# Expert gate rows and closing-norm vectors: spread over partitions by TensorE products in place of broadcasting DMAs

## What is computed

```python
def _post_norm(x, out, gain, bias):
    return _layernorm(DEEPNORM_ALPHA * x + out) * gain + bias

for i in range(DEPTH):
    sh_a, sc_a, g_a, sh_f, sc_f, g_f = _ada(c, w_ada[i], b_ada[i])   # c_ctx for the context tokens
    h = _modulate(x, sh_a, sc_a)
    ...                                                              # out: attention or Fourier mixing
    x = _post_norm(x, g_a * out, ln_gain[i, 0], ln_bias[i, 0])
    h = _modulate(x, sh_f, sc_f)
    moe = _hier_moe(h, w_router_group[i], w_router_expert[i], w_expert_gate[i], w_expert_up[i], w_expert_down[i])
    x = _post_norm(x, g_f * moe, ln_gain[i, 1], ln_bias[i, 1])
```

## Time and profile before

| | |
|---|---|
| median of 3 runs | 975.96 us (973.7 to 977.57) |
| profiled execution, span from first to last instruction | 968.9 us |
| PE, DVE, ACT, POOL busy | 821.1, 339.3, 147.5, 176.8 us |
| DMA | 321.39 MB, mean 332 GB/s |
| layer 0's pairs | from 320 us |
| layer 1's pairs | from 702 to 928 us |

### The profile page before, as it was taken

One profiled execution on the slowest core, in us unless ns is written; L12 is line 12 of the kernel. 1 busy time (PEld: TensorE's weight loads), 2 busy tenths in 40 slices (PEclk: granted clock), 3 DMA queues, 4 the chain that ended last, 5 costly groups with the idle time before them and its releaser, 6 DMA issues. The chain is left out here.

```text
span 968.9 us, 12777 instructions
## 1 busy us (share of the span) xinstructions
PE 821.1 (85%) x4895; PEld 419.4 (43%) x4895; DVE 339.3 (35%) x818; ACT 147.5 (15%) x339; POOL 176.8 (18%) x250
## 2 busy tenths in 40 slices
PE   3899999998898897998869788999599987777783
PEld 2555666665457433333323234546433333333331
DVE  3113554556587211111111137848611111101036
ACT  1122222223200111111101012001111110101013
POOL 2041212123122211122111100223212211111100
PEclk9999999999997999999999999999699999999998
DMA  9998493439339897999999979976899999999971
GB/s 333 365 371 305 140 386 112 167 135 342 145 105 387 353 412 290 420 420 418 419 418 419 418 304 356 381 264 230 353 387 418 417 419 418 419 419 420 419 297 65
DMA packets 91020, 321.39 MB, mean 332 GB/s; under 512 B 12686, under 2 KB 25710, under 8 KB 66872
## 3 DMA queue, kind: packets, MB, share of 16 engines
q1 hardware_dynamic: 74400, 289.41, 75.7%
q0 software_dynamic: 12704, 21.86, 6.3%
q10 hardware_dynamic: 3832, 8.99, 2.5%
HBM read 313.62 MB, written 28.90 MB: 354 GB/s over the span
## 5 line engine op out<-in xcount | busy, mean ns | idle before, releaser
L1067 PE MATMUL psum<-ring,arena 128*64 128x512 f32 x880 | 255.2, 629 | 39.1 <-DMA ring<-in_w_expert_up 28.4
L1067 PEld LDWEIGHTS psum<-ring,arena 128*64 128x64 f32 x880 | 84.8, 145 | 169.4 <-issue 166.0
L1089 PE MATMUL psum<-ring,arena 128*64 128x512 f32 x440 | 124.1, 598 | 20.2 <-DVE arena L1883 19.6
L1879 DVE TENSOR_TENSOR arena<-arena,psum 128x256 f32<-128x256 f32 x34 | 14.3, 421 | 283.6 <-ACT arena L1408 277.0
L1067 PE MATMUL psum<-h_hT,arena 128*64 128x512 f32 x208 | 93.1, 601 | 6.0 <-DMA ring<-in_w_expert_up 5.1
L937 PE MATMUL psum<-ring,h_hT 128*128 128x384 f32 x288 | 96.5, 488 | 0.0
L883 PE MATMUL psum<-ring,h_hT 128*128 128x512 f32 x160 | 69.3, 593 | 1.8 <-ACT h_hT L1489 1.5
L684 POOL DMA_INDIRECT y_scratch<-arena,sidx x32 | 33.6, 1048 | 203.9 <-DVE arena L1889 203.9
L937 PEld LDWEIGHTS psum<-ring,h_hT 128*128 128x128 f32 x288 | 53.6, 191 | 34.1
L1089 PEld LDWEIGHTS psum<-ring,arena 128*64 128x64 f32 x440 | 35.6, 136 | 71.2 <-issue 46.8
L1889 DVE COPY arena<-psum 128x512 f32<-128x512 f32 x32 | 22.1, 692 | 120.6 <-PE psum L1089 120.6
(11 more groups left out here) (230 smaller groups left out, 890.0 us busy)
## 6 DMA issues: line engine op xcount, KB each, us to landing
ring<-in_w_expert_down SPq DMA_DIRECT2D x52, 1024.0 KB, 20.6
ring<-in_w_expert_gate SPq DMA_DIRECT2D x50, 1024.0 KB, 19.0
ring<-in_w_expert_up SPq DMA_DIRECT2D x50, 1024.0 KB, 22.2
ring<-in_w_ada SPq DMA_DIRECT2D x24, 2048.0 KB, 15.0
h_hT<-in_w_expert_gate SPq DMA_DIRECT2D x12, 1024.0 KB, 20.4
h_hT<-in_w_expert_up SPq DMA_DIRECT2D x12, 1024.0 KB, 24.0
h_hT<-in_w_expert_down SPq DMA_DIRECT2D x12, 1024.0 KB, 26.5
ring<-in_w_qkv SPq DMA_DIRECT2D x9, 1024.0 KB, 12.5
```

Of the source, the lines that this page charges most:

```text
L1067: last = pe.matmul(bank[b][64 * e:64 * e + 64, :].rearrange("p (g n) -> p g n", g=2), mem.GT[b][:, c, 64 * e:64 * e + 64], w, start=(c == ...
L1089: last = pe.matmul(bank[5 + half][64 * e:64 * e + 64, :], mem.actT[b][:, f, 64 * e:64 * e + 64], w[:, f, 512 * half:512 * half + 512], sta ...
L1879: V.tensor_tensor(mem.act[b], mem.sil[b], bank[b][:, FE:2 * FE], ALU.mult).then_inc(S["act"], 1)
```

## The change

Per layer, the four 512 KB broadcasts go. POOL fetches the two gate rows (`fetch_gates`) and ScalarE the gain and bias as eight rows of 512 numbers into eight partitions of memory that is free by then (`mem.vectors`); both wait for the layer's last normalised rows (`norm_ready`). In pairs 4 to 11 TensorE runs one more product, with row r of an 8 by 8 identity, repeated 128 times, as the stationary side: it puts row r of the eight on all 128 partitions of bank 7. ScalarE copies bank 7 to its place in `gates` or `gb`. Also, gathers and scatters of the regular passes take their row numbers straight from the tables, without copy and wait; those of the extra passes keep both.

```diff
+        self.vectors = self.lnscale[0:8, TOK:TOK + 512]
...
             def gather(S, l, col, n, b):
-                pool.tensor_copy(mem.gidx[:, b:b + 1], mem.tokens[:, bass.ds(col, 1)]).then_inc(S["gidx"], 1)
-                n1 = value(n + 1)
-                pool.wait_ge(S["gidx"], n1)
+                if b == 2:
+                    pool.tensor_copy(mem.gidx[:, b:b + 1], mem.tokens[:, bass.ds(col, 1)]).then_inc(S["gidx"], 1)
+                    n1 = value(n + 1)
+                    pool.wait_ge(S["gidx"], n1)
+                    rows = mem.gidx[:, b:b + 1]
+                else:
+                    rows = mem.tokens[:, col:col + 1]
...
+            def fetch_gates(l):
+
+                pool.wait_ge(norm_ready, 6 * l + 6)
+                for i in range(2):
+                    pool.dma_start(mem.vectors[2 * i:2 * i + 2, :], m_dram[l, i, 5 * D:6 * D].rearrange("(h n) -> h n", h=2)
+                                   ).then_inc(gate_rows_in, 16)
...
                 if l == 0:
-                    pool.wait_ge(proj_used, 6)
-                    for i in range(2):
-                        spread(mem.gates[:, i, :], 0, 5, i, gates_in[i])
+                    fetch_gates(0)
...
                     if n < LAST:
                         gt(S, n + 1, 16 * ((n + 1) // 2 + 1), 1 - b)
+                    if 0 <= n - FIRST_SPREAD < VECTORS:
+                        spread_vector(VECTORS * l + n - FIRST_SPREAD)
                     act_transposes(S, n, b)
...
+                def spread_vector(v):
+
+                    pe.wait_ge(gate_rows_in, 32 * (l + 1))
+                    pe.wait_ge(norm_vectors_in, 32 * (l + 1))
+                    if v >= 1:
+                        pe.wait_ge(spread_sb, v)
+                    r = v % VECTORS
+                    pe.matmul(bank[7], bc(ident[0:VECTORS, r:r + 1], [VECTORS, P]), mem.vectors, start=True, stop=True
+                              ).then_inc(spread_ps, 1)
...
-                load_norm(2 * l + 1)
+                act.wait_ge(norm_ready, 6 * l + 6)
+                for i, name in enumerate(("ln_gain", "ln_bias")):
+                    act.dma_start(mem.vectors[4 + 2 * i:6 + 2 * i, :], A[name][l, 1].rearrange("(h n) -> h n", h=2)
+                                  ).then_inc(norm_vectors_in, 16)
...
                         gt_evict(S, n + 1, 1 - b)
+                        if 0 <= n - FIRST_SPREAD < VECTORS:
+                            vector_evict(n - FIRST_SPREAD)
                         o_evict(S, n, b)
...
             def gates_of_slots(l):
-                for i in range(2):
-                    dve.wait_ge(gates_in[i], 16 * (2 * l + 2))
+                dve.wait_ge(spread_sb, VECTORS * (l + 1))
```

More of the change, by code:

```diff
@@ L345, in build @@
         gate_up_through, down_through = sem("gate_up_through"), sem("down_through")
+        gate_rows_in, norm_vectors_in, spread_ps, spread_sb = (
+            sem(n) for n in ("gate_rows_in", "norm_vectors_in", "spread_ps", "spread_sb"))
         dve_chain, pool_chain = sem("dve_chain"), sem("pool_chain")
         def moe_sems(tag, fetches):
-            names = ("sidx", "gidx", *fetches, "gt_ps", "gt_act", "gt_dve", "u_ps", "sil", "act", "at_ps", "at_sb", "d_ps",
+            names = (*(("sidx", "gidx") if tag == "extra" else ()), *fetches, "gt_ps", "gt_act", "gt_dve", "u_ps", "sil", "act", "at_ps", "at_sb", "d_ps",
                      "o_act", "o_dve", "scattered", "o_free")
@@ L389, in build @@
         OFFSET_BANKS = (4, 0)
+        FIRST_SPREAD, VECTORS = 4, 8
         SUM_BANKS = (((2, 3), (4, 7), (0, 1)), ((2, 3), (0, 1), (6, 7)))
@@ L665, in gather @@
             def gather(S, l, col, n, b):
-                pool.tensor_copy(mem.gidx[:, b:b + 1], mem.tokens[:, bass.ds(col, 1)]).then_inc(S["gidx"], 1)
-                n1 = value(n + 1)
-                pool.wait_ge(S["gidx"], n1)
+                if b == 2:
[5 more added lines that the diff above has]
+                    rows = mem.tokens[:, col:col + 1]
                 pool.sem_inc(turns, 1)
                 pool.indirect_dma_start(mem.G[b], None, h_dram[l],
-                                        bass.IndirectOffsetOnAxis(ap=mem.gidx[:, b:b + 1].bitcast(U32), axis=0),
+                                        bass.IndirectOffsetOnAxis(ap=rows.bitcast(U32), axis=0),
                                         bounds_check=in_bound, oob_is_err=False
@@ L676, in scatter @@
             def scatter(S, l, col, n, b):
-                pool.tensor_copy(mem.sidx[:, b:b + 1], mem.table[:, bass.ds(col, 1)]).then_inc(S["sidx"], 1)
-                n1, n2 = value(n + 1), value(n + 2)
-                pool.wait_ge(S["sidx"], n1)
+                n2 = value(n + 2)
+                if S is extra:
+                    pool.tensor_copy(mem.sidx[:, b:b + 1], mem.table[:, bass.ds(col, 1)]).then_inc(S["sidx"], 1)
+                    n1 = value(n + 1)
+                    pool.wait_ge(S["sidx"], n1)
+                    rows = mem.sidx[:, b:b + 1]
+                else:
+                    rows = mem.table[:, col:col + 1]
                 pool.wait_ge(S["o_act"], n2)
@@ L684, in scatter @@
                 pool.indirect_dma_start(y_dram[l],
-                                        bass.IndirectOffsetOnAxis(ap=mem.sidx[:, b:b + 1].bitcast(U32), axis=0),
+                                        bass.IndirectOffsetOnAxis(ap=rows.bitcast(U32), axis=0),
                                         mem.O[b], None, bounds_check=out_bound, oob_is_err=False
@@ L1304, in head_evict, with load_norm @@
                 nc.scalar.copy(mem.hT[:, k, :], bank[3][:, 0:TOK]).then_inc(head_sb, 1)
[L1306 to L1309 removed]
+            def load_norm(l):
+                if l == 1:
+                    act.wait_ge(gb_used, 2)
                 for i, name in enumerate(("ln_gain", "ln_bias")):
[L1311 removed]
+                    act.dma_start(mem.gb[:, i, :], A[name][l, 0].partition_broadcast(P)).then_inc(gb_in, 16)
             for i, src in enumerate((A["c_ctx"].rearrange("(k p) -> k p", p=P),
@@ L1456, in first, with vector_evict @@
                         scale_rows()
+                def vector_evict(r):
+                    if r == 0:
+                        act.wait_ge(proj_used, 6 * l + 6)
+                        act.wait_ge(gb_used, 2 * l + 1)
+                    act.wait_ge(spread_ps, VECTORS * l + r + 1)
+                    dst, half = (mem.gates, mem.gb)[r // 4][:, r // 2 % 2, :], r % 2
+                    nc.scalar.copy(dst[:, 512 * half:512 * half + 512], bank[7]).then_inc(spread_sb, 1)
                 def body(n, b, r, k):
```

13 lines of the change are left out of this document (6 added, 7 removed).

## The result

| | before | after |
|---|---|---|
| median | 976.21 us (6 runs, 972.96 to 977.88) | 968.85 us (6 runs, 967.10 to 971.08) |
| ratio, 95% interval | | 0.9942 [0.9926, 0.9958] |
| profiled execution: span | 968.9 us | 968.7 us (its own time 970.48) |
| PE, DVE, ACT, POOL busy | 821.1, 339.3, 147.5, 176.8 us | 843.2, 341.3, 156.5, 162.3 us |
| DMA | 321.39 MB, mean 332 GB/s | 317.24 MB, mean 327 GB/s |

By the ratio the changed kernel gains 5.7 us (4.1 to 7.2); the two medians alone differ by 7.4. Forecast were 3.0 us, 973.0, in a range from 969.0 to 977.0. In a second comparison on another chip the ratio was 0.9947 [0.9928, 0.9965], 5.2 us (3.4 to 7.0), before 974.26 (22 runs), after 969.65 (6 runs). So the sign and the order were right.

What follows compares the result with a forecast made beforehand. Bound taken: a handshake of weight loads and TensorE, with DMA full inside the pairs but with holes elsewhere. Sum 1.08 + 1.92 + 0 + 0 = 3.0 us, 975.96 to 973.0, range 969.0 to 977.0.

Steps and rivals of the forecast that it cites:

- Holes, not bytes: Removed broadcasts, 4.19 MB, travel ahead of stretches where DMA runs low: directly they give nothing, only an earlier first gather.
- the microsecond that was named as the test: Prediction is wrong if the pair stages, from first full stretch to their end, change length by more than a microsecond.
- Bytes count: Rival, 6%: all 4.19 MB save time at 418 GB/s, 10.0 us, giving 966.0.
- Layer 1's start: TensorE's 1.92 us idle for layer 1's first gather goes whole; 1.26 kept as the lower end.
- lower bound of 1.26: Layer 1's first gather, issued at the copy's start with its old latency, lands 1.26 us earlier.
- Landing does not move: Rival, 14%: other weights fill the freed time and the gather lands as late as now; 0 to 1 us, about 975.5.
- Layer 0's start: TensorE's 1.08 us idle for layer 0's first gather goes whole, the gather being issued 1.26 us earlier.
- Overflow passes: Layer 0's pairs 0 to 2: first gather's saving is taken back by the second; 0 taken, bounds 0 to 1.0 us more.
- Products: Sixteen products in pairs 4 to 11 delay down products 0.43 to 0.6 us each, covered: 0 taken, 9.6 us uncovered.
- Moves with the work: Rise to full clock in layer 1's first gate_up shifts with the work, so the 1.92 us gain stays whole.
- Early clock: Rival, 16%: layer 1's first gate_up at full clock almost from its start, overflow keeps some saving; up to 6.8 us, 969.2.
- 7.1 us lie around the span: Base of the sum: median 975.96 against profiled span 968.9 us, the difference taken as unchanged.

Runs made afterwards that it cites:

- late_broadcasts: Kernel before without the regular index copies, each layer's four broadcasts asked for in pair 4 instead of at the layer's start; 979.72 us, ratio 1.0050 to before.
- norm_later: Kernel before with layer 1's gain and bias broadcasts asked for behind both first gathers, all bytes and copies kept; 974.40 us, ratio 0.9982.
- copies_only: Kernel before with the index copies of the regular passes removed, broadcasts kept; 973.32 us, ratio 0.9993 to before.
- spread_only: Changed kernel with the index copies and their waits put back, spread products kept; 970.86 us, ratio 0.9974 to before.

## Why the prediction was right, and where it was not

**Holes, not bytes.** Right. The pair stages kept their length within the microsecond that was named as the test: 0.5 us shorter in layer 0, 0.7 longer in layer 1's pairs 1 to 14 (198.4 against 197.6 and 197.8). 10.0 us of transfer left, 5 to 6 of time came, and late_broadcasts shows both prices of the same bytes. "Bytes count" is out.

**Layer 1's start.** Right in kind, 1.92 forecast, 2.4 measured: the rows came from an execution with a short wait (2.82 for the stage against 3.73 in the second profile). The floor behind it, TensorE's own chain through VectorE, was named and is what ends last now. The lower bound of 1.26 "from the new issue" was wrong twice: the request moves by 0.53 us, not 1.21 (the second gather's by 1.1 to 1.2, not 2), and moving it does not move the landing. "Landing does not move" is out, but for the copies alone it is what happens.

**Layer 0's start.** 1.08 forecast, 1.0 in the means, with a scatter as large: norm_later, whose layer 0 is that of before, shows 0.98 without any change. The prediction credited the copies; copies_only has 1.63 and spread_only 0.98, but beside norm_later's 0.98 a single profile of each does not settle which half it is, or whether it is the change at all.

**Overflow passes.** Here a term failed: "I take 0, since the later wait is the one that ends last". The first gather's wait did fall, and the second's did not rise to take it back:

```profile
378.34 1.16 PE L1067 MATMUL psum<-k_rows_sb,arena 128*128 128x128 f32 x8 [0.19 <-DMA arena<-h_scratch,gidx]
```

0.19 after, 0.21 before. The gather of the extra pass keeps its copy, but one of a scatter ahead of it on POOL's queue is gone: it is asked for 3.70 us after the gate and up products ahead of that wait begin, and 4.18 before. About 0.4 us, up to the 1.0 of the bound.

**Products.** Right that they are covered; the price of one was too low (0.88, not 0.43 to 0.6), which cost nothing.

**Clock.** "Moves with the work" holds at layer 1's start: 9.59, 9.87 and 8.94 us for the first gate_up in the three profiles after, 9.83 and 8.98 before. "Early clock" is out.

**End of layer 0.** This had no term and is the largest miss. From pair 14 to the Fourier products six profiles with one or two spread products in layer 0 take 39.36 to 41.01 us, mean 39.9; seven without take 40.50 to 43.03, mean 41.5. The kernel without products moves the same bytes as the changed one and is among the seven, which speaks for the products and against the bytes, by one profile. The difference lies behind SyncE's request for the experts' sums: up to it both groups take 18.8 to 19.3 us (norm_later 20.57), and from it to the Fourier products 20.5 to 20.6 with products (21.75 in the changed kernel's second profile) against 21.2 to 22.8 without. In that second part six of the seven profiles without have a while at half speed, and none of the six with them. First the kernel with four copies and the one without products,

```profile
585.53 3.55 PE L1147 MATMUL psum<-x,k_rows_sb 128*128 128x512 f32 x4 [3.08 <-DVE x L1946]
```

```profile
595.95 3.39 PE L848 MATMUL psum<-ring,silu 128*32 128x128 f32 x64 [2.46 <-DMA ring<-in_w_ada]
```

then the same products in the third profile of the changed kernel:

```profile
587.26 1.98 PE L1169 MATMUL psum<-x,k_rows_sb 128*128 128x512 f32 x4 [0.38 <-DVE x L1982]
...
595.31 1.95 PE L848 MATMUL psum<-ring,silu 128*32 128x128 f32 x64 [0.92 <-DMA ring<-in_w_ada]
```

The granted clock over the first two is 0.54 and 0.56, over the others 1.00; in the six it lengthens the products in this place by 1.4 to 1.8 us, as much as the two means differ. The seventh, the second profile of before, has none and takes 21.2; there, as in three more without products, the last of the sums lands 11.0 to 11.2 us after the first request and not 9.9 to 10.4. So the step that is missing is the clock, which the prediction followed at layer 1's start alone. Why the half speed falls into this place in one group and only ahead of it in the other, and whether the products or chance put it there, was not settled.

**Layer 1 behind its start** gave back about 0.9 us; with profiles of before 0.8 apart there, that stays open. Adding 0.5 for layer 1's start, 0.4 to 1.0 for the overflow passes and 0.8 to 1.6 for the end of layer 0 to the forecast 3.0, and taking off that 0.9, gives 3.8 to 5.2, from just under the first measured interval (4.1 to 7.2) to the lower half of it, and inside the second (3.4 to 7.0).

**Base.** "7.1 us lie around the span" was wrong: 1.8 us do. The rest was the luck of the profiled execution ahead of the experts. The difference did not use it, but the waits of that execution stood for typical ones.

## What to carry to other kernels

Before counting a saved transfer, look for the next stretch in which the DMA engines run dry: bytes ahead of it buy only what an event behind them (here a gather) gains, and the same bytes inside a full stretch buy their whole time. A small indirect transfer behind a loaded queue lands when the load has drained; asked for 0.5 us earlier or 0.7 later, it came at the same moment here, so take away what stands ahead of it. Moving it behind won the start as well, but in the total that did not show (norm_later). Where weights bound a stage, TensorE work put into it is free up to the wait that it replaces, and that limit is found by running it two and four times. And where a sum of waits leaves a microsecond or two over, compare the granted clock of the same products in both kernels.

## What the hardware showed that was not expected

**The clock falls behind products of eight rows, with TensorE busy.** With four products in a pair the granted clock goes to half (1.2 of 2.4 GHz) behind them in each of layer 0's pairs 4 to 11, and with two in pairs 4, 5, 8 and 10, although TensorE has no idle around them beyond waits of half a microsecond. With one it stays at 1.00 through pair 4 in two profiles of the changed kernel and falls in the third (below: the changed kernel, its third profile, then two products, then four):

```profile
417.00:419.00 2.00, 2.00 (x12) 1.00 1.00 402
```

```profile
418.60:420.60 2.00, 2.00 (x8) 0.68 (x6) 0.00 (x0) 0.00 (x0) 0.00 (x0) 0.50 1.04 418
```

```profile
416.00:418.00 2.00, 2.00 (x6) 1.00 1.03 424
418.00:420.00 2.00, 1.48 (x5) 0.68 1.04 414
420.00:422.00 2.00, 2.00 (x8) 0.50 1.01 426
```

```profile
418.00:420.00 2.00, 2.00 (x4) 0.50 1.05 420
420.00:422.00 2.00, 2.00 (x4) 0.50 1.00 414
```

(The columns are the stretch, its length, TensorE's busy time, in the second block also that of the other engines, then clock, DMA share, GB/s.) The down products behind four of them take 4.9 to 6.3 us instead of 3.65. A fall in the pairs is not peculiar to such products: the kernel before has three between layer 0's pairs 3 and 14, at the end of waits for weights of 2.5 to 3.1 us. And that the eight rows are the reason is not shown, since no run has full products of the same length in this place. The Trainium skill (TensorE: Matmul & The Clock Gate, The HAM clock gate) ties the clock to how busy the engine has been; in these rows it is busy by the profile and the clock falls all the same, so the busy time of the profile is not enough to forecast it.

**A gather waits for bytes on other queues.** The Trainium skill (DMA: Bandwidth & Descriptors, Queues, rings and completion order) says that a DMA engine goes round between the queues that have work, packet by packet. By that alone a gather on POOL's queue should pass a megabyte on ScalarE's; in the runs it landed 2.4 us (against the second profile of before 3.3 us) earlier when that megabyte was asked for behind it.
